# Expert rows through DRAM buffers, wide modulation steps and turned attention outputs in a two-layer diffusion trunk

## The reference

```
def trunk_layer(x, mod, g1, g2, lp, ffn, ctx):
    sh1, sc1, gt1, sh2, sc2, gt2 = mod
    mix, new_ctx = token_mixer(rmsnorm(x, g1) * (1 + sc1) + sh1, lp, ctx)
    x = x + gt1 * mix
    x = x + gt2 * ffn(rmsnorm(x, g2) * (1 + sc2) + sh2)

def modulation(cond, w_mod, b_mod):
    m = (jax.nn.silu(cond) @ w_mod + b_mod).reshape(-1, 1, 6 * D_MODEL)

def moe_swiglu(h, router, wg, wu, wd):
    logits = (h @ router).astype(jnp.float32)
    top_v, top_i = lax.top_k(logits, TOP_K)
    w = jax.nn.softmax(top_v, axis=-1)
    gate = jnp.sum(jax.nn.one_hot(top_i, N_EXPERTS) * w[..., None], axis=-2)
    for e in range(N_EXPERTS):
        y = y + gate[..., e:e + 1] * swiglu(h, wg[e], wu[e], wd[e])
```

## Time and profile before

| | |
|---|---|
| three runs, us | 1728.66, 1735.00, 1737.08 |
| median, us | 1735.0 |
| the profiled execution: time, span, us | 1735.82, 1734.0 |
| mean granted TensorE clock | 0.961 |
| TensorE / VectorE / ScalarE / GpSimd busy | 94% / 18% / 13% / 5% |
| bytes moved | 477.87 MB, mean 276 GB/s |

### The profile page before, as it was taken

One profiled execution on the slowest core, in us unless ns is written; L12 is line 12 of the kernel. 1 busy time (PEld: TensorE's weight loads), 2 busy tenths in 40 slices (PEclk: granted clock), 3 DMA queues, 4 the chain that ended last, 5 costly groups with the idle time before them and its releaser, 6 DMA issues.

```text
span 1734.0 us, 42376 instructions
## 1 busy us (share of the span) xinstructions
PE 1631.4 (94%) x19898; PEld 1040.4 (60%) x19899; DVE 311.2 (18%) x759; ACT 218.8 (13%) x574; POOL 92.7 (5%) x148
## 2 busy tenths in 40 slices
PE   4999879999979999799999999999999999999994
PEld 1776547777757754655555555556556555555552
DVE  0265320000033741410100100100101101001003
ACT  1221410000021231200100100100101001001001
POOL 5031021000002210000000000000000000000000
PEclk7999889999989998699999999999999999999997
DMA  9558744444433662779999999899899899899970
GB/s 332 157 178 312 290 116 129 146 146 147 157 123 108 245 220 63 289 280 388 355 351 387 338 371 388 318 389 386 321 386 391 317 385 382 327 386 337 369 288 26
DMA packets 210446, 477.87 MB, mean 276 GB/s; under 512 B 8726, under 2 KB 54454, under 8 KB 204118
## 3 DMA queue, kind: packets, MB, share of 16 engines
q1 hardware_dynamic: 206876, 469.32, 74.0%
q0 software_dynamic: 3392, 5.80, 1.1%
HBM read 473.21 MB, written 1.87 MB: 274 GB/s over the span
## 4 chain that ended last, share of the span: by engine, by line
PE 89%; DVE 5%; ACT 3%; issue 2%; DMA 1%; POOL 0%; DVEq 0%; POOLq 0%; ACTq 0%
PE ps L1106 34%; PE ps L1126 17%; PE ps L1013 9%; PE ps L714 7%; PE ps L1021 4%; PE ps L1003 3%; PE ps L669 2%; PE ps L1076 2%; PE ps L1083 2%; PE ps L1113 1%; PE ps L897 1%; DVE o_scratch L1514 1%; PE ps L701 1%; PE ps L761 1%; DMA cond_raw<-in_c 1%
## 5 line engine op out<-in xcount | busy, mean ns | idle before, releaser
L1106 PE MATMUL ps<-arena,scratch 128*32 128x256 f32 x10752 | 605.4, 380 | 0.7 <-ACT scratch L1421 0.7
L1106 PEld LDWEIGHTS ps<-arena,scratch 128*32 128x32 f32 x10752 | 342.3, 110 | 240.1 <-issue 21.5
L1126 PE MATMUL ps<-arena,scratch 128*32 128x256 f32 x5376 | 300.5, 379 | 5.0 <-ACT scratch L1238 5.0
L1126 PEld LDWEIGHTS ps<-arena,scratch 128*32 128x32 f32 x5376 | 173.9, 110 | 120.9 <-ACT scratch L1238 6.9
L1836 DVE TENSOR_TENSOR scratch<-scratch,ps 128x128 f32<-128x128 f32 x168 | 48.4, 288 | 782.7 <-ACT scratch L1430 782.7
L714 PE MATMUL ps<-arena,hT 128*128 128x256 f32 (+1 forms) x704 | 156.8, 382 | 6.2 <-issue 6.2
L1013 PE MATMUL ps<-hT,arena 128*128 128x256 f32 x704 | 158.0, 383 | 3.0 <-issue 3.0
L1013 PEld LDWEIGHTS ps<-hT,arena 128*128 128x128 f32 x704 | 135.5, 193 | 30.8 <-issue 13.0
L714 PEld LDWEIGHTS ps<-arena,hT 128*128 128x128 f32 x704 | 133.0, 193 | 25.1 <-issue 7.5
L1430 ACT ACTIVATE scratch<-ps 128x128 f32<-128x128 f32 x168 | 46.7, 278 | 801.7 <-PE ps L1106 801.7
L556 POOL TENSOR_TENSOR stat<-stat,half_neg 128x1 f32<-128x1 f32 x10 | 8.3, 834 | 1409.1 <-DVE stat L1909 1025.9
(11 more groups left out here) (339 smaller groups left out, 888.5 us busy)
## 6 DMA issues: line engine op xcount, KB each, us to landing
arena<-in_moe_w_gate SPq DMA_DIRECT2D x112, 1024.0 KB, 8.4
arena<-in_moe_w_up SPq DMA_DIRECT2D x112, 1024.0 KB, 10.4
arena<-in_moe_w_down SPq DMA_DIRECT2D x112, 1024.0 KB, 13.8
arena<-in_w_mod SPq DMA_DIRECT2D x48, 1024.0 KB, 7.0
arena<-in_w_in SPq DMA_DIRECT2D x20, 1024.0 KB, 5.5
arena<-in_ffn_w_gate SPq DMA_DIRECT2D x11, 1024.0 KB, 5.4
arena<-in_ffn_w_up SPq DMA_DIRECT2D x11, 1024.0 KB, 7.9
arena<-in_ffn_w_down SPq DMA_DIRECT2D x11, 1024.0 KB
```

Of the source, the lines that this page charges most:

```text
L1106: ins = mm(ps[32 * g:32 * g + 32, 4 + i % 3, 0:256], e_h[:, kt, 32 * t:32 * t + 32], gate_up_pair(u, kt, g), start=(kt == 0), stop=(kt == ...
L1126: ins = mm(y_part(q, t), e_hidT[:, g, 32 * t:32 * t + 32], arena[:, at + QUARTER * q:at + QUARTER * q + QUARTER], start=(first and t % 2 = ...
```

## The change

Three things are changed.

The experts' rows go through two buffers in DRAM. Once the routing is known, VectorE works out, for each token and each of its two experts, a row number (slot) in `slot_in` and `slot_out` (`find_slots`). GpSimd writes every token's row to its two slots by indirect DMAs. For experts 1 to 7 it loads 96 rows into `e_rows` (in `o_scratch`), and TensorE turns them with eight transposes (`gather_turn`) where the gather stood; expert 0 keeps the gather. Each expert's result rows are stored to `slot_out` by GpSimd, and in the last expert two indirect reads per stream bring every token its two rows, which VectorE weights and adds (`join_slots`). Only the last expert's rows still go through the weighted selection and `scatter`, after the loop. In layer 0 GpSimd fills the buffers with zeros.

The modulation steps have 32 stationary columns, the two vectors repeated 16 times, and write whole quadrants.

In the attention groups VectorE divides the probabilities by their sums before they are turned. `attention_out` makes v stationary (64 columns) and moves the turned probabilities, pairs of heads in two halves of the array, so that the output is already turned; VectorE copies it into `hT` (`attention_keep`), and `mix_turn` has four transposes per stream instead of eight.

```diff
-        mixed = sb("mixed", [P, D])
+        mixed = sb("mixed", [P, 768])
-        cond = sb("cond", [P, NS, KT])
+        cond = sb("cond", [P, KT, 16, NS])
+        e_rows = o_scratch[0:CAP].rearrange("p a n -> p (a n)")
+        NO_SLOT = E * CAP
...
     # GpSimd, opening: one more memset
-                                              (half_neg[:], -0.5), (ones2[:], 1.0)]):
+                                              (half_neg[:], -0.5), (ones32[:], 1.0), (mixed[:], 0.0)]):
...
     # GpSimd, layer 0, after the state store and before rstd
+                if layer == 0:
+                    for j in range(E):
+                        pool.dma_start(io["slot_in"][j * CAP * D:(j + 1) * CAP * D].rearrange("(p n) -> p n", p=P), mixed[:])\
+                            .then_inc(slots_zeroed, 16)
+                    pool.dma_start(io["slot_out"][(E - 1) * CAP * D:E * CAP * D].rearrange("(p n) -> p n", p=P), mixed[:])\
+                        .then_inc(slots_zeroed, 16)
...
     # GpSimd, after the layers
+            pool.wait_ge(slots_ready, 1)
...
+            for s in range(NS):
+                for k in range(2):
+                    g.indirect_dma_start(slot_in, bass.IndirectOffsetOnAxis(ap=slot_w[:, 2 * s + k:2 * s + k + 1].bitcast(U32), axis=0),
+                                         row[:, s, :], None).then_inc(slots_in, 16)
+            pool.wait_ge(slots_in, 64)
+            for e in range(1, E):
+                if e > 1:
+                    pool.wait_ge(gather_done, e)
+                pool.dma_start(e_rows, slot_in[e * CAP:(e + 1) * CAP, :]).then_inc(rows_in, 16)
+                pool.wait_ge(y_copied_act, e + 1)
+                pool.wait_ge(y_copied_dve, e + 1)
+                pool.dma_start(slot_out[(e - 1) * CAP:e * CAP, :], e_y[0:CAP, :]).then_inc(y_stored, 16)
+            pool.wait_ge(y_stored, 16 * (E - 1))
+            for s in range(NS):
+                for k, to in enumerate((f_y, row)):
+                    g.indirect_dma_start(to[:, s, :], None, slot_out, ...).then_inc(y_back, 16)
...
     # TensorE
-                        key, left = ("mod", layer, third, step - 1), cond[:, :, step - 1]
+                        key, left = ("mod", layer, third, step - 1), cond[:, step - 1].rearrange("p r s -> p (r s)")
-                        ins = mm(ps[32 * q:32 * q + 2, 7, :], left, right, start=(step == 0), stop=(step == KT))
+                        ins = mm(ps[32 * q:32 * q + 32, 7, :], left, right, start=(step == 0), stop=(step == KT))
...
-                pe.wait_ge(a_probs, ai + 1)
+                pe.wait_ge(a_normed, ai + 1)
...
-                for h in range(H):
+                for pair in range(2):
                     for t in range(1 + s):
-                        ins = mm(ps[:, b + 1, 64 * h:64 * h + 64], a_pT[s][:, t, h, :], v[t][:, h * nh // H, :],
-                                 start=(t == 0), stop=(t == s))
+                        for k in range(2):
+                            h = 2 * pair + k
+                            ins = mm(ps[64 * k:64 * k + 64, b + 1, P * pair:P * pair + P], v[t][:, h * nh // H, :],
+                                     a_pT[s][:, t, h, :], start=(t == 0), stop=(t == s), skip_group_check=True)
...
+            def gather_turn(e):
+                pe.wait_ge(rows_in, 16 * e)
+                for kt in range(KT):
+                    ins = turn(ps[:, 2 + kt // 4, P * (kt % 4):P * (kt % 4) + CAP], e_rows[:, P * kt:P * kt + P],
+                               ident[0:CAP, 0:CAP])
+                ins.then_inc(gather_done, 1)
...
     # TensorE, expert
                             pe.wait_ge(y_copied_act, e + 1)
                             pe.wait_ge(y_copied_dve, e + 1)
-                            scatter(0)
...
-                        else:
-                            pe.wait_ge(y_added, e * 2 + 2)
-                            scatter(1)
...
-                        if u == 3:
+                        if u == 3 and e == E - 1:
...
-                    gather()
+                    if e + 1 < E:
+                        gather_turn(e + 1)
                     turn_hidden(e, UNITS - 1, tiles)
                     unit_down(e, UNITS - 1, tiles)
...
     # ScalarE and VectorE, expert, before the copies of the result rows
+                        if e:
+                            act.wait_ge(y_stored, 16 * e)
...
     # VectorE, attention
-                dve.wait_ge(a_out, 4 * layer + 2 * kind + s + 1)
+                dve.wait_ge(a_probs, 4 * layer + 2 * kind + s + 1)
...
-                v.tensor_tensor(heads(pj(s, ("mcq", "aq")[kind]), H), heads(ps[:, b + 1, 0:256], H), last(inv, 64),
-                                ALU.mult).then_inc(a_mixed, 1)
+                v.tensor_tensor(a_p[s], a_p[s], last(inv, P * (1 + s)), ALU.mult).then_inc(a_normed, 1)
...
     # VectorE, expert
-                                if u == 0 and t < NS:
-                                    dve.wait_ge(scatter_done, e * 2 + (t + 1))
-                                    v.tensor_tensor(f_y[:, t, :], ps[:, 2:4, :]..., f_y[:, t, :], ALU.add).then_inc(y_added, 1)
+                            if e == 0 and u == 0:
+                                find_slots()
+                            if e == E - 1 and 2 <= u < 6:
+                                join_slots((u - 2) // 2, (u - 2) % 2)
...
+                    def join_slots(s, k):
+                        dve.wait_ge(y_back, 64)
+                        if k == 0:
+                            v.tensor_scalar(f_y[:, s, :], f_y[:, s, :], stat[:, 52 + s:53 + s], None, ALU.mult).then_inc(y_joined, 1)
+                        else:
+                            v.scalar_tensor_tensor(f_y[:, s, :], row[:, s, :], stat[:, 54 + s:55 + s], f_y[:, s, :],
+                                                   ALU.mult, ALU.add).then_inc(y_joined, 1)
```

More of the change, by code:

```diff
@@ L903, in mix_turn @@
                 pe.wait_ge(a_mixed, 4 * layer + 3 + s)
-                for kt in range(KT):
-                    ins = turn(ps[:, 3 * s + kt // 4, P * (kt % 4):P * (kt % 4) + P], mixer_out(s, kt), ident)
+                for k, name in enumerate(("gv", "rv")):
+                    for j in range(2):
+                        ins = turn(ps[:, 3 * s, 2 * P * k + P * j:2 * P * k + P * j + P],
+                                   pj(s, name)[:, P * j:P * j + P], ident)
                 ins.then_inc(mix_turned, 1)
@@ L990, in out_project @@
             def out_project(layer):
-                pe.wait_ge(mix_kept, NS * layer + 2)
+                pe.wait_ge(a_mixed, 4 * layer + 4)
                 pe.wait_ge(mix_kept_act, NS * layer + 2)
@@ L1661, in attention_norm, with attention_keep @@
                 link(v.reciprocal(inv, total))
-                v.tensor_tensor(heads(pj(s, ("mcq", "aq")[kind]), H), heads(ps[:, b + 1, 0:256], H), last(inv, 64),
-                                ALU.mult).then_inc(a_mixed, 1)
+                v.tensor_tensor(a_p[s], a_p[s], last(inv, P * (1 + s)), ALU.mult).then_inc(a_normed, 1)
+            def attention_keep(layer, s, kind):
+                kt = (2, 6)[kind]
+                dve.wait_ge(a_out, 4 * layer + 2 * kind + s + 1)
+                v.tensor_copy(hT[:, kt:kt + 2, P * s:P * s + P],
+                              ps[:, 3 * s + 1, 0:2 * P].rearrange("p (k t) -> p k t", k=2)).then_inc(a_mixed, 1)
             def mixers_two(layer):
@@ L1704, in mixers_two @@
                         attention_max(layer, s, kind)
+                    for s in range(NS):
+                        attention_norm(layer, s, kind)
                     dve.wait_ge(a_p_turned, 4 * layer + 2 * kind + 2)
@@ L1707, in mixers_two @@
                     for s in range(NS):
-                        attention_norm(layer, s, kind)
-                for s in range(NS):
-                    dve.wait_ge(mix_turned, n + s + 1)
-                    v.tensor_copy(hT[:, 4:8, P * s:P * s + P], ps[:, 3 * s + 1, :].rearrange("p (k t) -> p k t", k=4))\
-                        .then_inc(mix_kept, 1)
+                        attention_keep(layer, s, kind)
             for layer in range(L):
@@ L1863, in _ @@
+                    dve.wait_ge(slots_zeroed, 16 * (E + 3))
                     select(0)
[L1864 to L1865 removed]
                     dve.wait_ge(gather_done, 1)
@@ L1940 @@
         io[name] = nc.dram_tensor(f"out_{name}", shapes[name], F32, kind="ExternalOutput").ap()
+    slots = depth and inputs["moe_w_gate"].shape[1] * CAP
+    io["slot_in"] = nc.dram_tensor("slot_in", ((slots + 4 * P) * d,), F32, kind="Internal").ap()
+    io["slot_out"] = nc.dram_tensor("slot_out", ((slots + 1) * d,), F32, kind="Internal").ap()
     hybrid_step(nc, io)
```

112 lines of the change are left out of this document (69 added, 43 removed).

## The result

The changed kernel takes 1692.46 us (median of four runs, 1689.84 to 1699.24) against 1731.86 us for the kernel before, run beside it (1728.66 to 1737.08): 0.976 of the time, with a 95% interval of 0.974 to 0.979. I had forecast 1685 us, in a range of 1669 to 1713: 50 us less than the median of 1735.0 that I had then, where 39.4 were measured. The profiled execution of the changed kernel took 1690.85 us, with a span of 1688.9 us against the 1684.3 us of my sum.

A forecast was written before the change was run, and what follows sets the result against it. TensorE was taken to bound the expert loop, with the DMA weight stream within 6% of it. The terms summed as 1734.0 - 55.7 + 7 - 1 = 1684.3 us of span, 1685 us against the median; range 1669 to 1713 us.

The forecast's parts named there:

- TensorE's side of the loop: Expert loop: shorter seams, no scatters or selection turns take 55.7 us off TensorE; period falls from 121.98 to 115.14 us.
- The stream's side: Expert loop: weights plus rows, 44.83 MB per expert at 385 GB/s, take 116.4 us against TensorE's 115.14; stall about 7 us.
- 9.1: Expert loop: the stream needs 1.3 us more than TensorE's period per expert, 9.1 us over seven experts.
- 5.4: Last expert: its indirect reads add four times 512 KB, 2.1 MB, to the stream, 5.4 us.
- 7.8: Expert loop: reserve before TensorE waits; gate blocks asked for 16.2 us ahead land after 8.4, so 7.8 us can be lost.
- rival (b): Expert loop: row traffic costs the stream 2 to 4%, stalls of 15 to 40 us, 1693 to 1718 us; chance 0.20.
- Rival (a): Expert loop: TensorE stays the bound and no weight is late, 1678 us; chance 0.22.
- Rival (c): Modulation steps: wide steps keep the clock up where it falls beside them, some 8 us less, 1677 us; chance 0.08.
- Rival (d): Expert loop: GpSimd's row transfers beside the load queue slow the whole weight stream, 34 us more than now, 1769; chance 0.05.
- Rival (e): Slot path: something unseen (late rows, a blocked VectorE) gives most of the gain back, 1727 to 1743 us; chance 0.04.
- Attention: Attention stages: dividing first +6.0 us, paired outputs 5.5 less, fewer closing transposes 1.9 less; net taken as -1, bounds -4 and +4.
- Wide steps: Modulation steps with 32 stationary columns in place of 2: the load hides behind the matmuls, counted as zero.

## Why the prediction was right, and where it was off

**TensorE's side of the loop: right, a little low.** Seam 1.90 us against 2.1; no scatters but the last two; period without waits 115.1 as forecast beside the stream, and 114.5 where the stream is out of the way. The loop without waits would be 923.4 - 3.0 = 920.4 us; I had 924.4. These 4 us were gained, and lost again to the stream.

**The stream's side: right in mechanism, mis-sized.** The term was "Stall: 9.1 + 5.4 - 7.8, about 7 us". It measures 943.1 - 920.4 = 22.7 us, inside its bounds of 0 to 29. Set beside the run without row traffic, stretch by stretch, the first expert has none of it (108.2 us to the first `gather_turn`, against 108.4), the next six have 6 x 2.56 = 15.4, and the last has 7.5 (132.4 us from its `gather_turn` to the scatter, against 127.9 less 3.0 of waits). By the parts of the term:

- *9.1*, for seven experts at 1.3: it measures 117.08 - 114.52 = 2.56 per expert, 17.9 for seven. Half of the difference is the stream's side, 117.08 where I had 116.4: I priced the rows as ordinary bytes at 385 GB/s, and a second load of them costs nearly twice what as many weights cost. The other half is TensorE's shorter period, 114.52 where I had 115.14.
- *5.4* for the reads in the last expert: 4.32 us of wait, and 6.44 - 3.66 = 2.78 more because the block behind the wait ran at a lower clock. I had no term for the second.
- *The writes of the rows*, another 2.1 MB in the first expert, stand nowhere in the sum. I named them only as four indirect writes "with about 90 us to spare" for the rows' arrival, and forgot that they take the stream's time as the reads do: 5.4 us, as an estimate from their bytes at 387 GB/s. With the first expert's rows they used up the *7.8* of reserve that I credited to the later experts, which fits a first expert without stall and a second with the full stall (117.01); moving the writes out of the stream gave the loop 3.4 us back. The 7.8 itself was reckoned on the gate blocks, which land 8.4 us after being asked for the earlier trace rows. All the waits are for up blocks, which are asked for right behind them and landed after 10.4 (the page of the kernel before, part 6), so by the same working it was some 2 us too large.

```profile
arena<-in_moe_w_up SPq DMA_DIRECT2D x112, 1024.0 KB, 10.4
```

With these, 17.9 + 5.4 + 5.4 + 2.8 - 7.8 = 23.7, and some 26 with the smaller reserve: estimates, where the 22.7 and its stretches are measured. This puts the mechanism with rival (b), the stream that binds harder (15 to 40 us of stall), at its near end. The time landed at 1692.5 and not higher because of what I missed on the other side: the 4 us above, 5 us ahead of the loop and 1.9 behind the last scatter. That these offset more than half of the mis-sized stall was luck. The span is 4.6 us above the forecast by these terms; the rest of the 7.5 by which the median is above it lies in the choice of execution, as the traced one is 1.6 us below the median and I had taken it to be 0.8 above.

**Rival (a)**, TensorE alone the bound, falls: it needs the rows to be free, and only without them does the loop come to 923.4 us. **Rival (c)**, the clock through the wide steps, falls with their undoing; there was a gain through the clock, but it goes with the attention (beside the old attention the wide steps came with 67.7 us in place of 69.9 in one trace, which stays open). **Rival (d)**, a second queue that drags the stream down, showed only as 386 GB/s falling to 383 (384 by ScalarE's queue) with doubled loads, far from the 367 from which it decides. **Rival (e)** did not show: TensorE never waited for the rows, and for VectorE at most 0.9 us at a time.

**The rule on memory bandwidth** that the forecast set aside stays set aside: "DMA: Bandwidth & Descriptors" of the Trainium skill, section "Specifications", lists about 358 GB/s as the limit of one core, and here 386 were sustained over 657 us. The same page's section "Bandwidth" gives that figure for each core when both cores that share the memory stream; this kernel runs on one.

**Attention: right in sum, with parts that offset each other.** Undoing it costs 2.3 us in the medians, within the spread; I had 1. In the traces the attention stages of the two layers, from the first scores to the output projection, shrink by 0.6 and 0.9 us; I had 1.4 for both. The outputs of all four places, each up to the next step's start, take 8.3 us where they took 16.2: 7.9 less, where I had 5.5; a lower clock at two of the places before is in this sum. At the same granted clock of 1.00 (TensorE's timeline, layer 1) 16 of them took 1.88 us before, from 635.08 to the next step at 636.96, and now take 0.97, from 637.23 to 638.20; so pairs overlap almost wholly, where I had taken two thirds:

```profile
636.96 1.04 PE L669 MATMUL ps<-arena,cond 128*2 128x512 f32 x8
```

```profile
637.23 1.04 PE L938 MATMUL ps<-arena 128*64 128x128 f32 x16
638.20 1.06 PE L707 MATMUL ps<-arena,cond 128*32 128x512 f32 x8
```

The fewer closing transposes gave 3.5 us, not 1.9. The added product stands ahead of the turn, as forecast: TensorE's waits there grow by 5.7 us in all, and I had 6.0. What I left out took the surplus back: behind a longer wait the turn itself can run at the lower clock (1.72 us in place of 1.09 in layer 0), which cost 2.3 us over the four places, and there are new waits of 1.7 us.

```profile
181.32 1.09 PE L886 MATMUL ps<-arena 128*128 128x128 f32 x8 [1.17 <-ACT arena L1360]
```

```profile
182.78 1.72 PE L924 MATMUL ps<-arena 128*128 128x128 f32 x8 [1.70 <-DVE arena L1707]
```

**Wide steps: right at nothing.** The zeroing and the slot path were priced at nothing too and not tested alone. No wait in the loop answers to the slot path. The zeroing is issued from 174 to 180 us, beside the attention of layer 0, and that stage is 0.6 us shorter than before; from its end to the same product in layer 1 (213.27 to 620.06 before, 212.68 to 619.56 now) the time is the same within 0.1 us. **The end: 1.5 us** from the two scatters back to back (1667.72 to 1675.88 against 1709.60 to 1719.25, where VectorE's next product starts), with 1.3 forecast; the other 1.7 us lie behind the last output store.

## What to carry to other kernels

When two resources stand within a few per cent of each other, time taken from one is worth only the distance to the other, so list every byte that the change adds to the second, the one-off transfers too; each of them used reserve that another term had counted on. Look then for a gap in the stream's schedule and move the transfers into it: that gave 3.4 us in the loop and 6.6 in the medians here for a few moved lines, while moving them within the saturated stretch gave nothing. Price traffic to a new buffer as unlike the stream's own until a run says otherwise.

## What the runs showed that I had not expected

- Reads of a row buffer cost 4.4 to 4.9 us per MB in a saturated stream, the same bytes of weights 2.3, on the software queue, and the rows no less on ScalarE's hardware queue. The price stands in the DMA packets: 216 ns for 4 KB of rows and 166 for 4 KB of weights.
- The block behind a short wait of TensorE can run at the lower clock: blocks that take 3.66 us at full clock took 5.35 behind waits of 2.04, 2.43 and 2.91 us, but not behind others of 2.01, 2.28 and 2.57. Behind all twelve waits of 3.61 to 5.20 us in these loops the next block was slow. In mid-loop this seems to cost little: with three more slow blocks (5.35 us each) the loop with rows twice on GpSimd's queue was as long as that on ScalarE's (954.7 and 954.0 us), which fits a loop that waits for the stream.
- A shorter attention stage changes the clock of the stage behind it: the same 64 products took 27.73 us in the eleven traces with the new attention and 29.43 in the three with the old, that of before among them.
